# Dense feed-forward of a hybrid decoder step: the down projection rewritten as three products of rounded and low halves

## The reference

```
def _swiglu(h, wg, wu, wd):
    return (jax.nn.silu(h @ wg) * (h @ wu)) @ wd

D_MODEL = 1024
D_FF = ((8 * D_MODEL // 3 + 127) // 128) * 128     # 2816
x = x + _swiglu(h2, P['ffn_w_gate'][i], P['ffn_w_up'][i], P['ffn_w_down'][i])
```

## Time and profile before

| | us |
|---|---|
| median of 3 runs (lowest, highest) | 1846.82 (1846.73, 1847.57) |
| the profiled execution: span, first to last instruction | 1844.9 |
| TensorE busy in it | 1671.4 |
| VectorE busy | 1306.2 |
| ScalarE busy | 926.0 |
| GpSimd busy | 248.1 |

### The profile page before, as it was taken

The page is one execution under the profiler, slowest core; times in us unless marked ns, Lnnn a source line. Parts: engine busy times, 40 slices in busy tenths (PEclk is TensorE's granted clock), DMA queues, the critical chain, the costliest instruction groups (busy, mean ns, idle before and its releaser), DMA issues.

```text
span 1844.9 us, 31414 instructions
## 1 busy us (share of the span) xinstructions
PE 1671.4 (91%) x11268; PEld 1512.7 (82%) x11268; DVE 1306.2 (71%) x1743; ACT 926.0 (50%) x1229; POOL 248.1 (13%) x132
## 2 busy tenths in 40 slices
PE   6948799989998966789988999999999999999997
PEld 6838786889987965777787979798998979798895
DVE  3798845454401397983536989889898989889896
ACT  4432102244301532211225868777787868778784
POOL 4645310000002553521000000000000000000000
PEclk8968889989999887898988999999999999999999
DMA  6522113265545342112334989989898989989892
GB/s 242 162 69 74 46 69 114 100 214 181 174 128 159 101 132 61 59 49 83 126 126 140 364 300 355 344 308 365 288 365 291 357 310 348 370 285 361 294 360 101
DMA packets 103843, 386.14 MB, mean 209 GB/s; under 512 B 11696, under 2 KB 11728, under 8 KB 103008
## 3 DMA queue, kind: packets, MB, share of 16 engines
q1 hardware_dynamic: 102096, 372.00, 57.1%
q0 software_dynamic: 1680, 13.20, 2.0%
HBM read 377.79 MB, written 7.37 MB: 209 GB/s over the span
## 4 chain that ended last, share of the span: by engine, by line
PE 76%; DVE 18%; ACT 2%; issue 2%; DMA 0%; POOL 0%; SPq 0%; DVEq 0%; ACTq 0%
PE psum L1163 52%; DVE c L816 8%; PE psum L1407 4%; PE psum L1441 3%; DVE qkv L842 2%; PE psum L1198 2%; PE psum L1379 2%; PE psum L1499 2%; PE psum L1381 2%; DVE hT L767 1%; PE psum L1332 1%; PE psum L1362 1%; PE psum L1267 1%; PE psum L1230 1%; PE psum L1206 1%
## 5 line engine op out<-in xcount | busy, mean ns | idle before, releaser
L1098 DVE TENSOR_TENSOR w_lo<-ring,w_hi 128x1024 fp32r<-128x1024 f32 x528 | 644.6, 1224 | 72.0 <-ACT w_hi L711 65.7
L711 ACT ACTIVATE w_hi<-ring 128x1024 fp32r<-128x1024 f32 x528 | 557.7, 1061 | 143.0 <-PE psum L1163 136.0
L1163 PE MATMUL psum<-w_hi,h_hi 128*96 128x256 f32 x1408 | 402.1, 286 | 5.5 <-DVE w_lo L1098 5.5
L1163 PE MATMUL psum<-w_hi,h_lo 128*96 128x256 f32 x1408 | 394.7, 280 | 0.0
L1163 PE MATMUL psum<-w_lo,h_hi 128*96 128x256 f32 x1408 | 393.7, 280 | 0.0
L1163 PE MATMUL psum<-hid_hi,w_hi 128*128 128x264 f32 x1024 | 305.6, 298 | 39.7 <-POOL w_lo L418 30.0
L1163 PE MATMUL psum<-hid_lo,w_hi 128*128 128x264 f32 x1024 | 299.8, 293 | 0.0
L1163 PE MATMUL psum<-hid_hi,w_lo 128*128 128x264 f32 x1024 | 298.9, 292 | 0.0
L1163 PEld LDWEIGHTS psum<-hid_hi,w_hi 128*128 128x128 f32 x1024 | 203.4, 199 | 45.7 <-POOL w_lo L418 30.9
L1163 PEld LDWEIGHTS psum<-w_hi,h_hi 128*96 128x96 f32 x1408 | 228.5, 162 | 8.7 <-DVE w_lo L1098 7.4
L418 POOL TENSOR_TENSOR w_lo<-ring,w_hi 128x1024 fp32r<-128x1024 f32 x68 | 167.3, 2468 | 477.8 <-ACT w_hi L531 477.8
(11 more groups left out here) (280 smaller groups left out, 2000.7 us busy)
## 6 DMA issues: line engine op xcount, KB each, us to landing
ring<-in_w_exp SPq DMA_DIRECT2D x528, 512.0 KB, 5.3
ring<-in_w_mixer SPq DMA_DIRECT2D x112, 512.0 KB, 3.6
ring<-in_w_ffn SPq DMA_DIRECT2D x66, 512.0 KB, 3.5
early<-in_s POOLq DMA_DIRECT2D x2, 2048.0 KB, 8.6
out_ss<-early POOLq DMA_DIRECT2D x2, 2048.0 KB, 6.9
xT<-in_xT SPq DMA_DIRECT2D x1, 1056.0 KB, 5.0
out_yT<-hT POOLq DMA_DIRECT2D x1, 1056.0 KB, 4.2
early<-in_dw_win POOLq DMA_DIRECT2D x2, 496.0 KB, 5.8
```

What stands on the lines that cost most here:

```text
L711: A(w_hi[:, (n_split + u) % SPLIT, :], ring[:, u % RING, :, :].rearrange("p k n -> p (k n)"), ACT.Copy).then_inc(hi_done, 1)
L1098: V.tensor_tensor(w_lo[:, (n_split + u) % SPLIT, :], ring[:, u % RING, :, :].rearrange("p k n -> p (k n)"), w_hi[:, (n_split + u) % SPLIT, ...
L1163: last = M(out, lhs[x], rhs[w], start=(start and n == 0), stop=(stop and n == 2))
```

## The change

The down projection's 22 units become split units like the others, and its activations are kept as two halves, `ffn_hi` (where act_all was) and `ffn_lo` (at the place of `early`, running on over `c` and the first part of `qkv`). TensorE takes three products in place of one for each of the 176 pairs (t, f); with t = 0 it waits block by block for ffn_lo in place of once for all 22. ScalarE's and VectorE's queues run through all 66 units; silu times up now goes back into the silu buffer in float32, ScalarE copies it to ffn_hi one step later and VectorE subtracts one more step later. The adds to the residual are put between the low parts in VectorE's queue. VectorE waits for layer 0's state outputs before its loop.

```diff
+EARLY_AT, WORK_AT = 78464, 132864
-        act_all = work[:, 0:6, :].rearrange("p a b -> p (a b)")[:, 0:FT * T].rearrange("p (f t) -> p f t", t=T)
+        ffn_hi = nc.alloc_sbuf_tensor_at("ffn_hi", [P, FT, T], F32R, offset=WORK_AT)
+        ffn_lo = nc.alloc_sbuf_tensor_at("ffn_lo", [P, FT, T], F32R, offset=EARLY_AT)
...
-        for section, i0, i1 in (("mix0", 0, N_PROJ_SPLIT), ("mix0", N_PROJ + N_MIX, N_LAYER), ("ffn", 0, 2 * FT),
+        for section, i0, i1 in (("mix0", 0, N_PROJ_SPLIT), ("mix0", N_PROJ + N_MIX, N_LAYER), ("ffn", 0, N_FFN),
...
-                    for u in range(1, 2 * FT + 2):
-                        if u < 2 * FT:
-                            high_part("ffn", u)
-                        if u % 2 == 0 and u >= 4 or u == 2 * FT + 1:
-
-                            f = (u - 4) // 2 if u < 2 * FT + 1 else FT - 1
+                    for u in range(1, N_FFN):
+                        high_part("ffn", u)
+                        if u % 2 == 0 and 4 <= u < 2 * FT + 4:
+
+                            f = (u - 4) // 2
                             act.wait_ge(units_used, base_ord["ffn"] + 2 * f + 1)
                             if f >= 3:
-                                act.wait_ge(act_done, f - 2)
+                                act.wait_ge(ffn_lo_done, f - 2)
                             A(silu_g[:, f % 3, :], psum[:, 2 * (f % 3), 0:T], ACT.Silu).then_inc(silu_done, 1)
+                        if u % 2 and 5 <= u < 2 * FT + 5:
+
+                            f = (u - 5) // 2
+                            act.wait_ge(act_done, f + 1)
+                            A(ffn_hi[:, f, :], silu_g[:, f % 3, :], ACT.Copy).then_inc(ffn_hi_done, 1)
...
-                    for u in range(1, 2 * FT + 2):
-                        if u < 2 * FT:
-                            low_part("ffn", u)
-                        if u % 2 == 0 and u >= 4 or u == 2 * FT + 1:
-                            f = (u - 4) // 2 if u < 2 * FT + 1 else FT - 1
-                            dve.wait_ge(silu_done, f + 1)
-                            dve.wait_ge(units_used, base_ord["ffn"] + 2 * f + 2)
-                            V.tensor_tensor(act_all[:, f, :], silu_g[:, f % 3, :], psum[:, 2 * (f % 3) + 1, 0:T], ALU.mult).then_inc(act_done, 1)
-                    for t in range(KD):
+                    def add_down(t):
+
                         if t % 4 == 3:
                             dve.wait_ge(units_used, base_ord["ffn"] + 2 * FT + (t + 1) * FT // KD)
                         else:
...
+
+                    dve.wait_ge(state_out, 16 * 6)
+                    added = 0
+                    for u in range(1, N_FFN):
+                        low_part("ffn", u)
+                        if u % 2 == 0 and 4 <= u < 2 * FT + 4:
+                            f = (u - 4) // 2
+                            dve.wait_ge(silu_done, f + 1)
+                            dve.wait_ge(units_used, base_ord["ffn"] + 2 * f + 2)
+                            V.tensor_tensor(silu_g[:, f % 3, :], silu_g[:, f % 3, :], psum[:, 2 * (f % 3) + 1, 0:T], ALU.mult).then_inc(act_done, 1)
+                        if u % 2 == 0 and 6 <= u < 2 * FT + 6:
+                            f = (u - 6) // 2
+                            dve.wait_ge(ffn_hi_done, f + 1)
+                            V.tensor_tensor(ffn_lo[:, f, :], silu_g[:, f % 3, :], ffn_hi[:, f, :], ALU.subtract).then_inc(ffn_lo_done, 1)
+                        if u - 2 * FT - 3 >= -(-(added + 1) * FT // KD):
+                            add_down(added)
+                            added += 1
+                    for t in range(added, KD):
+                        add_down(t)
                     dve.wait_ge(down_taken, KD)
...
-                            w = arrived("ffn", 2 * FT + i // KD)
-                        if i == 0:
-                            pe.wait_ge(act_done, FT)
+                            w = parts("ffn", 2 * FT + i // KD)
+                        if t == 0:
+                            pe.wait_ge(ffn_lo_done, f + 1)
                         if f == 0 and t >= 2:
                             pe.wait_ge(down_taken, t - 1)
-                        last = M(psum[:, 6 + t % 2, 0:T], w[:, i % KD, :], act_all[:, f, :], start=(f == 0), stop=(f == FT - 1))
+                        last = split_products(psum[:, 6 + t % 2, 0:T], [h[:, i % KD, :] for h in w], [h[:, f, :] for h in (ffn_hi, ffn_lo)], f == 0, f == FT - 1)
```

More of the change, by code:

```diff
@@ L268, in build @@
         act_done = sem("act_done")
+        ffn_hi_done = sem("ffn_hi_done")
+        ffn_lo_done = sem("ffn_lo_done")
         down_done = sem("down_done")
```

## The result

The changed kernel takes 1868.53 us (median of 4 runs, 1856.69 to 1877.10) against 1846.80 (1846.73 to 1847.57): ratio 1.011, 95% interval 1.0076 to 1.0143. It is slower where I forecast 1832.8 us.

The account below looks back on a forecast made before the run. TensorE's instruction pace was taken to bound the feed-forward. Products, seam, new wait and adds moved the down projection's end from 587.56 to 573.6 us, 14.0 earlier: 1846.8 - 14.0 = 1832.8 us, range 1830.4 to 1835.2 (eight in ten).

Parts of the forecast that it names:

- Products (part 1): Down projection: 528 split products at 120.8 ns, 2.900 us a unit, 63.8 us for 22 units; plain projection took 78.57.
- Column pace: Rival: down projection products at t > 0 go as fast as columns pass, 4.6 us less, 1828.2 us; chance 5%.
- lower clock: Rival: stalls drop the granted clock to 1.2 GHz in the down projection; up to 116 us more, 1885; chance 1%.
- The rule of the Trainium skill: Down projection products: columns / 2.4 GHz + 2.5 ns, 112.5 ns each, 59.4 us in all; rejected for the trace's 120.8 ns.
- Seam (part 2): Between gate and up and down projection: starting t = 0 on finished blocks removes TensorE's 0.85 us gap.
- New wait (part 3): Unit 46: TensorE stalls 1.1 us for block 21's late low half, 1.3 with slow first step; bounds 0 and 2.5.
- Adds (part 4): Down projection: residual adds between VectorE's low parts delay t = 4 by 0.2 us; bounds 0 and 1.0 us.
- Work on the other engines and transfers (parts 5 and 6): Feed-forward: extra VectorE and ScalarE work, weight loads and VectorE's wait for state outputs cost nothing.
- What follows is shifted as a whole: Everything behind the down projection comes 14.0 us earlier unchanged, allowing 1.3 us either way for the clock in the mixer.
- lag that grows: Rival: copies, low parts and adds fall behind, TensorE waits in each t; about 4 us back, 1837; chance 7%.

Follow-up runs that it names:

- a_fewest: Changed kernel without split_tile's waits that repeat one already made, 36 instructions less ahead of the job loop: 1833.28 us, ratio 0.9917.
- a_loop: Changed kernel with 11 fewer instructions inside the job loop (low-half waits for every second block only), head unmoved: 1846.40 us, 1838.58 to 1866.91 in 10 runs.
- b_pad64: Kernel before the change with 64 further do-nothing instructions ahead of TensorE's job loop: 1847.29 us in one run.
- a_best: a_fewest with VectorE taking block 21's low half ahead of the low part of unit 48: 1835.76 us, ratio 0.9921.
- a_pad158: Changed kernel with 158 further do-nothing instructions ahead of the router's products in TensorE's stream: 1845.21 us, ratio 0.9983.

## Why the prediction was wrong

**The parts on the feed-forward held.** *Products (part 1):* the copies of units 49 and 57 start at 518.69 and 542.03, 2.92 us a unit against 2.900 forecast, 0.4 us over 22 units. Column pace and the lower clock didn't come. The rule of the Trainium skill that part 1 holds against the trace ("TensorE: Matmul & The Clock Gate", section "Back-to-back issue gap") was no measure for this stream: the section gives it for a product by itself and says that it misses a stream of weight loads and products both ways. *Seam (part 2):* gone. *New wait (part 3):* forecast 1.1 us and a slow first step, measured (waits, 383 to 575 us; the other row is the one at the head of gate and up):

```profile
PE psum L1183 <- DVE ffn_lo L1020: 1.0, 1, 1.0
PE psum L1183 <- DVE w_lo L762: 0.7, 1, 0.7
```

*Adds (part 4):* forecast 0.2 us at t = 4; no wait is shown, but the copy released by the end of unit 55, the first of t = 4, is 0.23 us late:

```profile
542.03 1.06 ACT L535 ACTIVATE w_hi<-ring 128x1024 fp32r<-128x1024 f32 x1 [1.85 <-PE psum L1183]
545.18 1.06 ACT L535 ACTIVATE w_hi<-ring 128x1024 fp32r<-128x1024 f32 x1 [2.10 <-PE psum L1183]
```

*Work on the other engines and transfers (parts 5 and 6)* cost nothing. w_o of layer 1 starts at 910.03, forecast 909.5. The sum of these parts was 14.0 us; at the first job 13.56 are there.

**The step that failed** is the sentence behind the sum, "What follows is shifted as a whole", whose one allowance was the clock in the mixer. I priced each instruction where it runs, and not what 354 more of them do to the place of the code behind them. The only loop of TensorE in the kernel lies there and goes round eight times. Without its 38.9 us the profiled execution would be at 1833.2 us (1872.1 - 38.9); a_fewest, whose passages are clean, measures 1833.28. So the term left out, priced at nothing without a reason, is the whole error to within half a microsecond.

No rival of mine was this one. The *lag that grows* and the *lower clock* looked for a loss in the feed-forward. The profile of before did show the thing, in a row I didn't use: 48 code packets for a program with a loop of over 6 blocks that goes round eight times. All rounds but the first came from loaded code, and that was a condition that could be lost.

The Trainium skill has the mechanism, in "Runtime: NRT & Kernel Launch", section "Instruction fetch mechanics": code comes in 16 KiB blocks, read ahead in sequence, and a taken branch whose target has left the window must wait for a load. The trace agrees, with packets of 16 KB and a stop of 4.18 us. The same section gives TensorE 128 KiB, eight blocks. With that figure, reading ahead by one block leaves room for a loop that touches seven blocks and none for one that touches eight. The runs say the same without it. A loop of 6.4 blocks touches seven or eight by its place. If blocks begin at about .85 of my count, at a_loop's end (an estimate from the limit below), every clean kernel of the table touches seven and the four others eight. The clean ones load nothing again in any round; each miss of the others loads nine packets, the loop's eight and one more. So eight blocks stay and nine don't; the resident blocks themselves no run shows. Its other sentence, that the window is two blocks only, the kernel before contradicts: no packet in seven rounds of 6.4 blocks.

**What stays open.** The limit lies between ends of 49.80 (no miss) and 49.90 (six of seven) in my count, which starts at the program's first instruction and doesn't know what the runtime puts ahead of it. Why at this limit one passage misses and the next doesn't isn't shown; what the trace has is that the short passage lacks the first packet too, the one for the block behind the loop. Nor is why five or six misses cost 4.5 to 7.8 us each and not the same.

## What to carry to other kernels

A loop that is long against the engine's loaded code has a good and a bad place (shown here for TensorE alone), and any edit ahead of it moves it. Before pricing a change that adds or removes instructions of such an engine, count by how many blocks of 256 the loop moves; after a run, compare the count of code packets and the idle time put down to issue behind the branch. If they rose, take away or add a few dozen instructions ahead of the loop before judging the change: here the same arithmetic measures 1.011 of the old time or 0.992, by 36 redundant waits.

## What the runs showed that I had not expected

- One miss brings nine packets and costs 4.5 to 7.4 us in the changed kernel: 2.7 to 4.2 us of standstill, and 1.1 to 2.8 us more for the 24 products of the gather behind it (3.79 to 5.43 us in place of 2.65).
- A wait that is long fulfilled isn't free on TensorE in numbers: with 158 instructions of them the idle time in front of the router's products is 14.7 us, with 98 it is 8.0 us, 82 to 93 ns each. Since 5.8 us of waiting are there without any, the first 64 cost nothing that shows (b_pad64).
- The time has groups without any miss (a_best: 1831.2 and 1836, a_pad158: 1843 to 1845 and 1850.4). The kernel before has them too, though its first four runs didn't show it: of 48 later ones 39 took 1845.81 to 1849.22 us and eight 1855.25 to 1856.20 (one more, at 7039.13, is left out of all ratios). Between the profiles of a_fewest and a_best a difference stands in layer 0's mixer, 260 to 310 us, in that order, in the granted clock (0.80, 0.73). A w_o that starts at 344.23 in the one starts at 348.28 in the other; at the first job 1.8 us of these 4 are left (988.43, 990.26). What makes the groups isn't shown. The rows of a_fewest and then of a_best:

```profile
260.00:310.00 50.00, 47.34 (x192) 34.70 (x192) 20.28 (x34) 10.74 (x22) 8.16 (x3) 0.80 0.21 73
```

```profile
260.00:310.00 50.00, 47.77 (x193) 34.66 (x192) 19.32 (x35) 8.12 (x19) 8.16 (x3) 0.73 0.15 55
```
